# Five groups of constant fp32 products on TensorE replaced by groups of fp32r products that read converted weights

## What is computed

```python
for layer in range(DEPTH):
    mix = mixer(rms_norm(h, norm_pre), ...)
    h = h + rms_norm(mix, norm_post)
    ff = squared_relu_mlp(rms_norm(h, mlp_norm_pre[layer]), mlp_w_up[layer], mlp_w_down[layer])
    h = h + rms_norm(ff, mlp_norm_post[layer])

def squared_relu_mlp(h, w_up, w_down):
    u = jax.nn.relu(h @ w_up)
    return (u * u) @ w_down
```

## Time and profile before

| | |
|---|---|
| median of 3 runs | 965.85 us (965.27 to 966.38) |
| span of the profiled execution | 963.2 us |
| TensorE matmul busy | 952.3 us, 99%, 7530 records |
| TensorE weight load busy | 909.1 us, 94% |
| VectorE busy | 748.2 us, 78% |
| ScalarE busy | 547.7 us, 57% |
| GpSimd busy | 89.4 us, 9% |
| DMA | 166.6 MB, mean 173 GB/s |
| chain that ended last | PE 82%, DVE 12%, issue 2%, ACT 2%, DMA 2% |

### The profile page before, as it was taken

How to read it: one execution, slowest core, us unless ns; L and a number is a source line. 1 busy time by engine, 2 the same in 40 slices (tenths; PEclk the granted TensorE clock), 3 DMA queues, 4 the chain that set the end, 5 groups by cost and what they waited for, 6 DMA issues and landing times.

```text
span 963.2 us, 18430 instructions
## 1 busy us (share of the span) xinstructions
PE 952.3 (99%) x7530; PEld 909.1 (94%) x7530; DVE 748.2 (78%) x1129; ACT 547.7 (57%) x819; POOL 89.4 (9%) x91
## 2 busy tenths in 40 slices
PE   9999999999999999999999999999999999999998
PEld 8999999999999998999999999999999999999998
DVE  6998778978855599867987844489887998787777
ACT  6652366656454476756665544455666665556455
POOL 5334101000201000001000201001001000000000
PEclk9999999999999999999999999999999999999999
DMA  8733444766666836436476575626636467665651
GB/s 256 243 120 115 143 128 140 218 200 197 195 183 193 267 109 197 150 113 183 136 215 197 176 214 184 194 68 182 183 110 202 127 197 214 187 190 170 203 175 44
DMA packets 164723, 166.62 MB, mean 173 GB/s; under 512 B 6784, under 2 KB 162832, under 8 KB 164640
## 3 DMA queue, kind: packets, MB, share of 16 engines
q1 hardware_dynamic: 162752, 163.47, 55.5%
q0 software_dynamic: 1056, 1.19, 0.5%
q10 hardware_dynamic: 832, 0.79, 0.4%
HBM read 163.82 MB, written 1.08 MB: 171 GB/s over the span
## 4 chain that ended last, share of the span: by engine, by line
PE 82%; DVE 12%; issue 2%; ACT 2%; DMA 2%; SPq 0%; POOL 0%; ACTq 0%; DVEq 0%
PE ps L657 19%; PE ps L660 16%; PE ps L649 13%; DVE w_lo L1990 4%; PE ps L676 3%; PE ps L677 3%; PE ps L678 3%; PE ps L682 2%; PE ps L683 2%; PE ps L684 2%; PE ps L689 2%; PE ps L609 2%; PE ps L617 2%; PE ps L690 2%; PE ps L691 2%
## 5 line engine op out<-in xcount | busy, mean ns | idle before, releaser
L1990 DVE TENSOR_TENSOR w_lo<-w_raw,w_hi 128x1024 fp32r<-128x1024 f32 (+4 forms) x314 | 375.0, 1205 | 116.1 <-ACT w_hi L1424 110.3
L1424 ACT ACTIVATE w_hi<-w_raw 128x1024 fp32r<-128x1024 f32 x298 | 313.3, 1056 | 200.3 <-PE ps L660 47.6
L657 PE MATMUL ps<-xs,w_hi 128*128 128x256 f32 x1012 | 132.6, 277 | 0.0
L657 PEld LDWEIGHTS ps<-xs,w_hi 128*128 128x128 f32 x1012 | 127.0, 188 | 4.5
L660 PE MATMUL ps<-xs,w_lo 128*128 128x256 f32 x832 | 112.2, 277 | 0.0
L660 PEld LDWEIGHTS ps<-xs,w_lo 128*128 128x128 f32 x832 | 102.9, 188 | 0.2
L682 PE MATMUL ps<-xs,w_hi 128*128 128x256 f32 x320 | 91.4, 285 | 0.4 <-DVE w_lo L1990 0.4
L683 PE MATMUL ps<-xs,w_hi 128*128 128x256 f32 x320 | 89.3, 279 | 0.0
L684 PE MATMUL ps<-xs,w_lo 128*128 128x256 f32 x320 | 89.3, 279 | 0.0
L649 PE MATMUL ps<-xs,w_hi 128*128 128x512 f32 x326 | 85.1, 393 | 0.3 <-DVE mo L2018 0.2
L1431 ACT ACTIVATE tmp<-ps 128x512 f32<-128x512 f32 x75 | 44.5, 593 | 70.6 <-PE ps L649 62.6
(11 more groups left out here) (431 smaller groups left out, 1896.6 us busy)
## 6 DMA issues: line engine op xcount, KB each, us to landing
w_raw<-in_mlp_w_up SPq DMA_DIRECT2D x64, 512.0 KB, 4.2
w_raw<-in_mlp_w_down SPq DMA_DIRECT2D x64, 512.0 KB, 3.5
w_raw<-in_a_w_in SPq DMA_DIRECT2D x32, 512.0 KB, 4.3
w_raw<-in_w_gate SPq DMA_DIRECT2D x22, 512.0 KB, 3.8
w_raw<-in_w_up SPq DMA_DIRECT2D x22, 512.0 KB, 4.6
w_raw<-in_w_down SPq DMA_DIRECT2D x20, 512.0 KB, 4.4
w_raw<-in_w_kv SPq DMA_DIRECT2D x16, 512.0 KB, 4.3
w_raw<-in_w_in SPq DMA_DIRECT2D x16, 512.0 KB, 3.9
```

The lines of the kernel that those rows point to most:

```text
L657: mm(ps[:, 2 * pset + n, at], hi[:, kk, n * P:(n + 1) * P], x[:, kt0 + kk, at], start=False, stop=False)
L1424: o = fn(dst, raw, ACT.Copy)
L1990: return v.tensor_tensor(d, x, y, ALU.subtract)
```

## The change

The calls `keep_streaming(4, B7)` ahead of up0 and `keep_streaming(6)` ahead of ak0, up1, cq and pg are replaced by calls of a new function. It waits until both parts of the next matrix' first unit are converted, and then issues seven products for each entry of a list. All are fp32r. The stationary operand is a slice of `w_hi` of that unit's first part (a new 128-column slice for each of the seven, or the same one where the third field is True), of 128, 64 or 32 columns; the moving operand is a slice of `w_hi` of its second part: 256, 384 or 512 columns in a row, the same from an offset of 4 or 16 columns, two halves apart, pairs taken from two places in turn, or 512 columns of `w_lo`. They write to the same bank as before, which nothing reads.

```diff
@@ -824,6 +824,31 @@
             def keep_streaming(n, bank=B6):
                 for _ in range(n):
                     mm(ps[:, bank, 0:S], ident, table[:, T_IDENT:T_IDENT + S], start=True, stop=True)
+
+            def stream_shapes(name, shapes, bank=B6):
+
+                s0, s1 = slot_of(UNIT0[name], 0), slot_of(UNIT0[name], 1)
+                pe.wait_ge(lo_ready, 2 * UNIT0[name] + 2)
+
+                def moving(kind):
+                    row = w_hi[:, s1, :]
+                    if kind == "halves":
+                        return row.rearrange("p (a t) -> p a t", a=4)[:, 0:3:2, :]
+                    if kind == "pairs":
+                        return row[:, 0:512].rearrange("p (a t) -> p t a", a=2)
+                    if kind == "back":
+                        return row[:, 511::-1]
+                    if kind == "low":
+                        return w_lo[:, s1, 0:512]
+                    at, n = kind
+                    return row[:, at:at + n]
+
+                for kind, cols, one in shapes:
+                    x = moving(kind)
+                    n = kind[1] if isinstance(kind, tuple) else 512
+                    for j in range(7):
+                        at = 0 if one else P * j
+                        mm(ps[0:cols, bank, 0:n], w_hi[:, s0, at:at + cols], x, start=True, stop=True)
 
             pe.wait_ge(blank_ready, 1)
             for _ in range(5):
@@ -993,7 +1018,7 @@
             sums("a_post")
             keep_streaming(1)
             bucket_rows()
-            keep_streaming(4, B7)
+            stream_shapes("up0", (((0, 512), P, False), ((0, 512), P, True)), B7)
             stream("up0", xs, pairs=16, waits=xs_wait("m0"), two=True, after=lambda: pe.wait_ge(rel_copied, 1))
 
             def us_wait(first):
@@ -1002,7 +1027,7 @@
                 return w
             stream("down0", us, per=4, waits=us_wait(0), last_kt=FF // P - 1, first_pair=lambda: sums("m0_pre"))
             sums("m0_post")
-            keep_streaming(6)
+            stream_shapes("ak0", (((4, 512), P, False), ((16, 512), P, False)))
 
 
             pe.wait_ge(pair_summed, PAIR0["b_out"])
@@ -1096,11 +1121,11 @@
             stream("b_out", xs_b, waits=xs_wait("attn"), two=True,
                    between={1: last_pairs, 4: lambda: turn_pair(3)})
             sums("b_post")
-            keep_streaming(6)
+            stream_shapes("up1", (((0, 512), 64, False), ((0, 256), 64, False), ((0, 256), 32, False)))
             stream("up1", xs, pairs=16, waits=xs_wait("m1"), two=True)
             stream("down1", us, per=4, waits=us_wait(16), last_kt=FF // P - 1, first_pair=lambda: sums("m1_pre"))
             sums("m1_post")
-            keep_streaming(6)
+            stream_shapes("cq", ((("halves"), P, False), (("low"), P, False)))
 
 
             pe.wait_ge(p_in, 16)
@@ -1332,7 +1357,7 @@
                    mid=lambda: sums("f_pre"), two=True)
             stream("down2", us, per=3, waits=us_wait(32), last_kt=FF2 // P - 1, first_pair=lambda: sums("ple"))
             sums("f_post")
-            keep_streaming(6)
+            stream_shapes("pg", (((0, 384), P, False), ("pairs", P, False)))
 
             def turn_last():
                 pe.wait_ge(xs_ready, XS0["last"] + KT)
```

## The result

| | before | changed |
|---|---|---|
| median, us | 966.0 (965.14 to 966.7) | 967.54 (966.34 to 968.3) |
| ratio | 1 | 1.0015, interval 1.0008 to 1.0022 |
| span of the profiled execution, us | 963.2 | 965.0 |

A forecast was written before the change was run, and what follows sets the result against it. TensorE's issue was taken as the bound (matmul row 99% busy, clock full), with short stretches where VectorE leads. The five seams sum as 1.47 + 0 + 0 + 0 + 0 = +1.5 us, median 967.3, range 965.3 to 969.0.

The forecast's parts named there:

- Seam 1: Ahead of up0: the new filler is 1.47 us longer and no wait is left to hide it; +1.47 us.
- Seams 2 and 3: Ahead of ak0 and up1: fillers of 3.20 and 3.19 us are covered by waiting for tile 1's low half; nothing.
- Seam 4: Ahead of cq: first L617 0.26 us late, absorbed by a later 0.5 us wait for POOL; cost nothing.
- Seam 5: Ahead of pg: the new filler takes 2.80 us and ends before L609's wait for ScalarE's xs does; cost nothing.
- The spacing as it was: Behind the seams: 256-column products keep the 113 or 118 ns spacing each stretch had before; no change counted.
- rival (a): Seam 5 turns to slow spacing, or covers in seams 3 and 5 fall short: 0.5 to 0.8 us more; chance 0.20.
- What would show it: Signs in the trace: seam 1's first L617 1.4 to 1.5 us late, 512-wide fillers 0.229 us apart; another spacing refutes.
- (b): New products cost as fp32 ones, 0.43 us for 512 columns: +12.9, 979; strided entry alone +1.2, 968.5; chance 0.07.
- (c): Slow stretches behind seam 1, seam 3 or both turn fast: +0.6, +0.4 or -0.4 us in all; chance 0.28.
- (d): Clock drops behind a seam because 64 or 32 stationary columns leave most of the array unused: 969 to 973; chance 0.02.
- (e): Seam 1 has cover that the prediction doesn't see: 965.9; chance 0.05.
- The difference between span and median: Whole kernel: profiled span 963.2 is 2.65 us under the median 965.85; taken as fixed, so span 964.7 gives 967.3.

The follow-up runs named there:

- seven-product runs: The two runs seam1_seven and seam1_fp32_seven, with seven products ahead of up0, of the new kind and in fp32: 965.92 and 967.47 us.
- seam1_only: Changed kernel with the old fillers put back ahead of ak0, up1, cq and pg, the new one only ahead of up0: 967.52 us, ratio 1.0016 to the kernel before.
- seam1_fp32_seven: Kernel before with seven fp32 products ahead of up0 in place of four: 967.47 us, ratio 1.0014.
- seams2to5_only: Changed kernel with the four old fp32 products put back ahead of up0, the other four places new: 965.83 us, ratio 0.9998 to the kernel before.
- seam1_seven: Changed kernel with only the first seven of the fourteen fp32r products ahead of up0: 965.92 us, ratio 0.9999 to the kernel before.

## Why the prediction was right, point by point

- **Seam 1, +1.47.** Right in mechanism and size: +1.40 by the shift, L617 1.49 further behind its data, and the two medians of seam 1 alone and the whole change both lie 1.5 us over the kernel before. The step that carried it, no cover left because L617 already followed its data at once, is shown by the seven-product runs: the same length in fp32 costs the same, the same kind at the old length costs nothing. That the tiles behind don't give it back is shown by the shift, which stays.
- **Seams 2 and 3, nothing.** Right: L617 within 0.05 us of its data, shift unchanged.
- **Seam 4, 0.26 late and absorbed.** Absorbed, yes: the shift is no larger at 667 than ahead of the seam. The forecast 0.26 counts from L617's old start at 638.55; from the data at 638.49 it is 0.32, and that compares with the 0.39 measured. The cover is the wait for POOL: 0.54 us in the kernel before, `seam1_only` and `seam1_fp32_seven`, which have the old filler at seam 4, and 0.34 to 0.36 in the changed kernel, `seams2to5_only` and `seam1_seven`.
- **Seam 5, 2.80 and covered.** The filler was covered (PE still waited 0.15). The two sizes were off in opposite ways, and the sum stayed near by luck: 216 ns for the strided 512 columns where I took 229, but 171 to 185 (178 on average) for 384 columns where I took 172. Seven of each at these spacings are 2.76 us. My bounds for the stride, 213 to 430, held it, near the lower end. I called L917's row the nearest: 114 ns for 128 columns in fp32, against 108 for half of an unstrided record. It showed that no large price was due, and didn't show the gain.
- **The spacing as it was.** Here the forecast was wrong in three small places: seam 5 came out slow (+0.38, rival (a), which I priced at 0.5), seam 1's slow stretch lasted some 5 us longer (+0.14), and something between 740 and 756 gave back 0.25. They come to +0.27 together, in one traced execution of each kernel. I said that I couldn't compute the state. The runs support that: kernels whose seam 5 or seam 1 was untouched differ from the kernel before in it, and six with the old filler at seam 5 are slow there. So (a)'s spacing came true, but its cause, the new filler, isn't shown and is unlikely. Nor do the times need it: the changed kernel's median is 1.54 over the kernel before, about what seam 1 alone costs. My forecast of the median was 0.24 low, of which 0.15 is that I started from 965.85, where more executions gave 966.0.
- **What would show it.** I wrote that the 512-wide fillers would stand 0.229 us apart and that another spacing would speak against me. Those in a row do on average (226 to 239 ns), the pairs at 215 to 216 don't. The difference lay under the cover of seam 5, so the time doesn't show it.
- **Rivals.** (b) fell: no shape of the change costs as fp32; behind the first of a group, the dearest spacing is 239 ns. (c) didn't happen: both stretches behind seams 1 and 3 stayed slow (1.18 at 176.15 and 472.69). (d) fell for the change, though its mechanism is real as soon as nothing is issued. (e) fell: no cover in seam 1.
- **The difference between span and median** was taken as fixed at 2.65. It is 967.54 - 965.0 = 2.54 in the changed kernel, near it by luck. Where an execution's time and its own span are both on record, the time is about 1.8 us longer (966.79 and 965.0 for the profiled one). The rest is how far the profiled execution happened to lie under its median, 0.75 us here.
- The column count of the stationary side was costed at nothing. Right: 64 and 32 columns are 113 to 117 ns for 256 moving columns, and 227 to 239 for 512.

## What to carry to other kernels

A filler that keeps TensorE's clock up is free only up to the moment when the awaited data lands: read that moment beside the first product that needs it, and cut the filler there, whatever it is made of. It still must not be left out: here its absence costs four times what its excess does. And when a product is the bound, try the order in which its moving operand is read from memory before its count. Measure it, since pairs gained and fours lost; and let the writer write in a row and read by stride, since that way round cost little here.

## What of the hardware was unexpected

- fp32r products with a weight load each, 512 moving columns: 224 to 239 ns in a row, 215 to 216 in pairs 128 or 256 elements apart, 271 to 284 in fours 256 apart. The Trainium skill (TensorE: Matmul & The Clock Gate, Step-by-step: what each phase is for) says that loading the next weights takes no read bandwidth from the running product. The runs don't show what the 13 ns are, only that they hang on how the moving operand lies. The Trainium skill's formula of columns over 2.4 GHz and 2.5 ns (TensorE: Matmul & The Clock Gate, Back-to-back issue gap) gives, as an estimate, 216 ns for 512 columns and 109 for 256. The 216 of the pairs agrees; the 229 of the row and the 111.6 of 256 columns in pairs don't.
- The 113 and 118 ns of 256 columns are two spacings of the same product at full clock, and the slow one lasts 17 to 27 us. Behind one added product of 64 or 192 columns in down0, or 128 in down1, the slow stretch was gone; behind one of 320 in down1 it wasn't. What starts it is open.
- Without fillers the granted clock was halved at every seam, for 23.9 us together, though TensorE's one wait in each was only 1.6 to 3.0 us long.
